# Modulation jobs moved out of the first and last attention head, beside values and Fourier inputs

## What is computed

```python
def adaln(cond, w_mod, b_mod):
    m = jax.nn.silu(cond) @ w_mod + b_mod
    return jnp.split(m, 3, axis=-1)
...
def attn_fourier_layer(...):
    shift, scale, gate = adaln(c, w_mod, b_mod)
    h = rmsnorm(x, norm_g) * (1.0 + scale[:, None]) + shift[:, None]
    q, k, v, f, z = jnp.split(h @ w_in, SPLIT0, axis=-1)
    q = apply_rope(q.reshape(B, S, N_Q_HEADS, HEAD_DIM), cos, sin)
    ...
    y = jnp.concatenate([windowed_attention(q, k, v, kc, vc, sink), fourier_mix(f, w_f)], axis=-1)
    x = x + gate[:, None] * ((y * jax.nn.silu(z)) @ w_out)
...
def pool_layer(...):
    shift, scale, gate = adaln(c, w_mod, b_mod)
    h = rmsnorm(x, norm_g) * (1.0 + scale[:, None]) + shift[:, None]
    x = x + gate[:, None] * pool_branch(h, w_in, w_grp, layer_scale, w_out)
```

## Time and profile before

| | us |
|---|---|
| median of 3 executions | 1515.44 (1514.88 to 1517.31) |
| the profiled execution | 1516.59 |
| its span, first to last instruction | 1514.9 |
| PE busy | 1440.4 (95%) |
| DVE busy | 888.8 (59%) |
| ACT busy | 499.5 (33%) |
| mean granted clock of PE | 0.986 |

### The profile page before, as it was taken

The page is one execution under the profiler, slowest core; times in us unless marked ns, Lnnn a source line. Parts: engine busy times, 40 slices in busy tenths (PEclk is TensorE's granted clock), DMA queues, the critical chain, the costliest instruction groups (busy, mean ns, idle before and its releaser), DMA issues.

```text
span 1514.9 us, 18270 instructions
## 1 busy us (share of the span) xinstructions
PE 1440.4 (95%) x6822; PEld 1166.2 (77%) x6822; DVE 888.8 (59%) x1389; ACT 499.5 (33%) x732; POOL 85.4 (6%) x159
## 2 busy tenths in 40 slices
PE   4799999999998999998999999999999999999995
PEld 0366888888877788877788888888888888888884
DVE  3643444436666868686755577655554666674433
ACT  3332332325544534344322244111252222332221
POOL 1000000000000000000010000000000000010001
PEclk9899999999999999999999999999999999999997
DMA  9777346545642333333475666533333322365322
GB/s 389 294 278 282 124 127 195 182 140 184 194 133 72 123 98 126 94 127 111 166 237 185 193 193 193 167 98 98 97 98 97 98 87 94 98 190 198 101 70 111
DMA packets 63684, 232.57 MB, mean 154 GB/s; under 512 B 7104, under 2 KB 8000, under 8 KB 62336
## 3 DMA queue, kind: packets, MB, share of 16 engines
q1 hardware_dynamic: 40896, 145.77, 29.3%
q0 software_dynamic: 21040, 80.42, 16.3%
q10 hardware_dynamic: 1680, 5.43, 1.0%
HBM read 227.40 MB, written 4.19 MB: 153 GB/s over the span
## 4 chain that ended last, share of the span: by engine, by line
PE 84%; DVE 9%; DMA 2%; issue 1%; ACT 1%; POOL 0%; DVEq 0%; SPq 0%; ACTq 0%; POOLq 0%
PE ps L1235 83%; DMA raw<-in_mod 2%; DVE w_lo L746 2%; PE ps L1447 1%; DVE stat L998 1%; DVE pt_lo L1019 1%; DVE tmp L846 1%; DVE modchunk L753 1%; DVE main L791 1%; DVE h_lo L798 1%; DVE h_lo L800 1%; DVE kvmem L874 0%; DVE kvmem L1025 0%; ACT scratch L507 0%; DVE main L849 0%
## 5 line engine op out<-in xcount | busy, mean ns | idle before, releaser
L1235 PE MATMUL ps<-h_hi,w_hi 128*128 128x512 f32 x1600 | 635.0, 397 | 6.5 <-DVE h_lo L800 5.9
L1235 PE MATMUL ps<-h_hi,w_lo 128*128 128x512 f32 x1600 | 625.8, 391 | 0.0
L1235 PE MATMUL ps<-h_lo,w_hi 128*128 128x512 f32 x1600 | 625.5, 391 | 0.0
L746 DVE TENSOR_TENSOR w_lo<-raw,w_hi 128x1024 fp32r<-128x1024 f32 x208 | 254.6, 1224 | 404.4 <-ACT w_hi L410 403.9
L410 ACT CAST w_hi<-raw 128x1024 fp32r<-128x1024 f32 x208 | 218.1, 1049 | 651.8 <-PE ps L1235 651.7
L1235 PEld LDWEIGHTS ps<-h_hi,w_hi 128*128 128x128 f32 x1600 | 302.6, 189 | 81.4 <-issue 22.3
L1235 PEld LDWEIGHTS ps<-h_hi,w_lo 128*128 128x128 f32 x1600 | 301.9, 189 | 64.2
L1235 PEld LDWEIGHTS ps<-h_lo,w_hi 128*128 128x128 f32 x1600 | 302.4, 189 | 60.1 <-issue 0.2
L753 DVE CUSTOM_DVE_ANT_0 modchunk<-modchunk,cond_row 128x1024 f32<-128x1024 f32 x128 | 155.3, 1219 | 2.5 <-DMA modchunk<-in_modb 2.5
L357 POOL DMA_DIRECT2D modchunk<-in_modb x128 | 67.6, 528 | 1171.8 <-DVE modacc L753 1138.7
L611 ACT CAST pt_hi<-ps 128x512 fp32r<-128x512 f32 (+1 forms) x48 | 30.7, 640 | 129.9 <-PE ps L1447 129.8
(11 more groups left out here) (199 smaller groups left out, 1378.1 us busy)
## 6 DMA issues: line engine op xcount, KB each, us to landing
raw<-in_weights SPq DMA_DIRECT2D x208, 512.0 KB, 3.5
modchunk<-in_modb POOLq DMA_DIRECT2D x128, 512.0 KB, 4.3
raw<-in_mod SPq DMA_DIRECT2D x44, 512.0 KB, 5.4
modchunk<-in_mod SPq DMA_DIRECT2D x20, 512.0 KB, 4.9
main<-in_xT POOLq DMA_DIRECT2D x4, 1024.0 KB, 13.3
kvmem<-in_weights POOLq DMA_DIRECT2D x8, 512.0 KB, 5.4
main<-in_xT ACTq DMA_DIRECT2D x4, 1024.0 KB, 4.8
out<-main SPq DMA_DIRECT2D x12, 256.0 KB, 3.1
```

Source lines behind the costliest of these rows:

```text
L746: nc.vector.tensor_tensor(w_lo[:, j % 2], src, w_hi[:, j % 2].bitcast(F32), ALU.subtract).then_inc(lo_ready, 1)
L1235: return nc.tensor.matmul(out, lhsT, rhs, start=start, stop=stop, skip_group_check=True)
```

## The change

On DVE the sets beside values and Fourier inputs become two each, so two jobs stand in each unit, one after the other, and the first and the last head have none. The sets keep their order. In the first head the third part of a rotation stands with the second, one slot earlier. In the last head the splits move, on ACT and on DVE, from behind the slot's cast to its end. The number of instructions of each kind stays as it was.

```diff
--- before.py
+++ after.py
@@ -64,7 +64,7 @@
 BANKS = ([LOWER, (6, 7, 4, 5), (2, 3, 0, 1), UPPER, LOWER, UPPER] + [LOWER] * 4 + [UPPER, LOWER] * 8)
 POOL_BANKS = (UPPER, LOWER, UPPER, LOWER)
 
-M_V, M_F, M_Q, M_Z, M_O, M_U, M_O1, M_END = starts(1, 1, 3, 4, 4, 1, 2)
+M_V, M_F, M_Q, M_Z, M_O, M_U, M_O1, M_END = starts(2, 2, 3, 2, 4, 1, 2)
 
 H_X, H_MIX0, H_L1, H_MIX1 = starts(2 * KT, KT, KT)
 
@@ -598,9 +598,6 @@
                     if k in UNIT_SLOTS:
                         s = UNIT_SLOTS.index(k)
                         hi(i + G_Z, s + 2)
-                        if last and 2 * s < EARLY:
-                            split(H_MIX0 + 2 * s, main[:, 2 * s], h_hi[:, 2 * s])
-                            split(H_MIX0 + 2 * s + 1, main[:, 2 * s + 1], h_hi[:, 2 * s + 1])
                     if k in QUERY_SLOTS:
                         n = QUERY_SLOTS.index(k) + 1
                         if n >= 2:
@@ -618,6 +615,9 @@
                     if first and k % 3 == 1 and k < 3 * GROUP:
                         m = k // 3
                         swap(3 * GROUP + m, main[:, 3 * GROUP + m], scratch, 3 * GROUP + m)
+                    if last and k in UNIT_SLOTS and UNIT_SLOTS.index(k) < EARLY // 2:
+                        for t in (2 * UNIT_SLOTS.index(k), 2 * UNIT_SLOTS.index(k) + 1):
+                            split(H_MIX0 + t, main[:, t], h_hi[:, t])
                     if last and k in (7, 10, 13):
                         reload_x((7, 10, 13).index(k))
                     if k == STEPS and not last:
@@ -762,17 +762,23 @@
                 nc.vector.tensor_tensor(modv_flat[:, bass.ds(cg * GROUP, GROUP)], modsum[:],
                                         vec[:, bass.ds(cg * GROUP + V_BMB, GROUP)], ALU.add).then_inc(modv_ready, 1)
 
-            def group(n, cg=None, finish=None, side=None, last=False):
+            def jobs(cg, sets, s):
+
+                for f in range(sets * s, sets * (s + 1)):
+                    job(cg + f // HALVES, f % HALVES)
+                    if f % HALVES == HALVES - 1:
+                        reduced(cg + f // HALVES)
+
+            def group(n, cg=None, finish=None, side=None, last=False, sets=1):
 
                 for s in range(HALVES - 1 if not last else HALVES - 2):
                     lo(n, s + 2)
                     if cg is not None:
-                        job(cg, s)
+                        jobs(cg, sets, s)
                     if side:
                         side(s)
                 if cg is not None:
-                    job(cg, HALVES - 1)
-                    reduced(cg)
+                    jobs(cg, sets, HALVES - 1)
                 if finish:
                     finish()
                 if not last:
@@ -956,8 +962,8 @@
             lo(G_K, HALVES + 1)
             dve.wait_ge(rope_landed, 32)
             dve.wait_ge(cond_row_ready, 2)
-            group(G_V, M_V, finish_values, side=rotate_beside(0, lambda m: keys[:, m]))
-            group(G_F, M_F)
+            group(G_V, M_V, finish_values, side=rotate_beside(0, lambda m: keys[:, m]), sets=2)
+            group(G_F, M_F, sets=2)
             nc.vector.memset(folded[:, :, 1, 0:1], 0.0)
             fold(0)
             fold(1)
@@ -1005,9 +1011,6 @@
                     if k in UNIT_SLOTS:
                         s = UNIT_SLOTS.index(k)
                         lo(i + G_Z, s + 2)
-                        if last and 2 * s < EARLY:
-                            split(H_MIX0 + 2 * s, main[:, 2 * s], h_hi[:, 2 * s], h_lo[:, 2 * s])
-                            split(H_MIX0 + 2 * s + 1, main[:, 2 * s + 1], h_hi[:, 2 * s + 1], h_lo[:, 2 * s + 1])
                     if k in QUERY_SLOTS:
                         n = QUERY_SLOTS.index(k) + 1
                         piece(i * PIECES + (5 + n), q_lo[:, n % 2],
@@ -1024,14 +1027,19 @@
                         p = probs[par][:, 0:width - 1]
                         nc.vector.tensor_scalar(p, p, stat[:, 3, par:par + 1], None,
                                                 ALU.mult).then_inc(probs_ready, 1)
-                    if k in JOB_SLOTS:
-                        job(i + M_Z, JOB_SLOTS.index(k))
+                    if k in JOB_SLOTS and not (first or last):
+                        job(i + (M_Z - 1), JOB_SLOTS.index(k))
+                    if last and k in UNIT_SLOTS and UNIT_SLOTS.index(k) < EARLY // 2:
+                        for t in (2 * UNIT_SLOTS.index(k), 2 * UNIT_SLOTS.index(k) + 1):
+                            split(H_MIX0 + t, main[:, t], h_hi[:, t], h_lo[:, t])
                     if first and 2 <= k:
                         m, part = divmod(k - 2, 3)
-                        rotate_part(3 * GROUP + m, main[:, 3 * GROUP + m], scratch[:], part)
+                        for turn in ((0,), (1, 2), ())[part]:
+                            rotate_part(3 * GROUP + m, main[:, 3 * GROUP + m], scratch[:], turn)
                     if k == STEPS and not last:
                         keys_and_first_queries(i + 1)
-                reduced(i + M_Z)
+                if not (first or last):
+                    reduced(i + (M_Z - 1))
                 dve.wait_ge(y_done, i * BLOCKS + BLOCKS)
                 if last:
                     lo(i + G_Z, HALVES + 1)
```

## The result

The changed kernel takes 1505.9 us (median of 4, 1504.6 to 1507.2) against 1515.9 us: the ratio is 0.9935, with a 95% interval from 0.9923 to 0.9947. The forecast was 1506.8 us. Its profiled execution took 1507.1 us, with a span of 1505.5. The gain is small, 0.65%, but clear of the noise.

The account below looks back on a forecast made before the run. TensorE (PE) was taken as the bound, busy nearly throughout. Heads -19.7 us and added work beside values and Fourier inputs +11.1 us give -8.6 us: median 1515.4 to 1506.8 us, range 1499.5 to 1514.5.

Parts of the forecast that it names:

- Swaps in the first head: First head: ACT's last three swaps no longer wait for DVE's add, so PE stalls shrink by 1.5, 2.65 and 2.0 us.
- The low part at slot 7 and the head's end: First head: PE's 0.58 us stall for the probabilities' low part and 1.33 us before the second head end: 0.6, 1.3 us.
- Splits in the last head: Last head: with splits behind the scaling, PE's waits for it fall from 5.0 to 1.25 us; a 0.8 us wait goes.
- Jobs behind the scaling worth nothing: Last head: the eight jobs leaving it stand ahead of maxima that PE does not wait for, so they gain nothing.
- The clock: First and last head: with large stalls gone, all 7.1 us lost at clock 0.96 are regained; the other end is zero.
- The values stage: Near 236 us: another job pair delays the first context-values copy, and PE waits for its bank, +1.9 us.
- The Fourier stage: Near 286 us: job pairs outlast units, lateness piles up, and PE waits for the second query unit's low part, +6.65 us.
- the cycle of a pair: Fourier stage: job start to issue 2.0 us plus landing 4.5 us, so 6.5 us against a unit of 5.44 us.
- The queues' share: Fourier stage: DMA queue use rises from 0.58 to 0.73, not full, which spoke against lengthening landings.
- Slow clock behind it: After the values and Fourier stalls: slow-clock stretches cost 0.8 and 1.75 us, together +2.55 us.
- D: Rival, chance 0.13: Fourier-stage landings lengthen under their own traffic; gain gone at 5.7 us, 1519.4 us at 6.3.
- B: Rival, chance 0.15: loads keep up, landing in 3.8 us, a pair in 5.8 us; added cost 4.45 us, time 1500.2 us.

## Why the prediction was right, step by step

- **Swaps in the first head**: -1.5, -2.65, -2.0 us forecast; the three stalls became 0, 0.43 and 0. Shown by the rotation part alone.
- **The low part at slot 7 and the head's end**: -0.6 and -1.3; both stalls are gone. The first went with the jobs alone and with the rotation part alone, so that either was enough; the forecast gave it to the job. Of the second, the rotation part alone left 1.18 of 1.33 us and the jobs alone left none, so there it was the job, not the add, that mattered.
- **Splits in the last head**: 5.0 to 1.25 us forecast, 0.9 measured. The quarter of a microsecond that I put on a wait coming back did not come. Shown by the splits alone.
- **Jobs behind the scaling worth nothing**: PE's wait for the scaling fell from 5.0 to 4.2 us with the jobs alone. In slots 2 and 8 of the kernel before the maximum starts right behind a job, and with the jobs alone DVE is idle for 0.6 us before it; the waits of 0.63 and 1.06 us behind these two became 0.20 and 0.65. The splits' move removes these waits by itself (0.9 us with the jobs still there), so the zero did no harm to the sum.
- **The clock**: 7.1 us forecast. Both heads had a clock of 1.00 in the first profile; in the second the first head had 0.98, one low stretch that cost 1.6 us. The sum holds within that; the reasoning "a stall of this size, so a slow stretch" is too simple. With jobs or rotation moved alone the last head kept stalls of 1.78 and 1.54 us at a clock of 1.00, and 1.79 us at the start of the first head brought a slow stretch in some kernels and none in others. What decides it stays open.
- **The values stage**: +1.9 forecast, 1.0 and 1.2 measured in two profiles of the changed kernel, 1.5 to 1.7 in others with two sets there.
- **The Fourier stage**: +6.65 forecast, 4.2 and 5.4 measured. The place, the waiting instruction and the cause were as said; the mis-sized term is the cycle of a pair, 6.2 us in the first profile and 6.4 in the second instead of 6.5. Over seven cycles 0.3 us are 2.1 of the 2.4 us by which the forecast was above the first profile. The cycle was issue and landing and nothing else: 1.9 us to the issue, where I took 2.0, and in the first profile a landing of 4.2 us on average, where I took 4.5. The median of all landings of the stage, 3.8, is lower than that, because the loads of the other half, which did not set the pace, were shorter on average. The queues' share, 0.73 forecast, was 0.73 and 0.70.
- **Slow clock behind it**: +2.55 forecast; a clock of 0.59 over 7 us is work lost for 2.9 us, and the stretch of the ledger less its two stalls gives 8.67 - 1.01 - 4.23 = 3.4 us, and 8.74 - 1.23 - 5.40 = 2.1 us in the second pair. The longer stall had the shorter slow stretch, so the whole row repeated to 0.1 us; no run shows why.
- **The rivals**: the balance of D needed landings of 5.7 us; the mean was 4.2 where it mattered. B needed a pair in 5.8 us; the median landing was as short as B had it, but those of the half that set the pace were not, so the stall stayed. The warning of the Trainium skill (SBUF — State Buffer, "SBUF: two separate sides") about descriptors held up by a DVE instruction that holds the shared port did not show; whether a job holds that port is in no row. POOL's issues took 0.53 us, and the landings behind them had a median of 3.8 us. The Trainium skill's formula for a load (DMA: Bandwidth & Descriptors, section "Anatomy of one DMA — SWDGE (gpsimd) path"), by which I estimated 3.2 us for 512 KB, lies below the 3.6 us of the shortest landing in that stage.

What the forecast did not ask was which part of the change earns the gain, though its own terms answer it: it charged 11.1 us to the moved jobs and gave them 1.9 us of stalls in the heads. The job moves, which the change is named for, cost 2.7 us by themselves (1518.3 against 1515.6) and 6.9 us on top of the two reorderings.

## What to carry to other kernels

On an engine that works in order, look at what stands ahead of the instruction that another engine's queue waits for: standing a 0.7 us add one slot earlier, for each of four tiles, gave 10 us. A swap that waited for the add had held up the instructions behind it that PE needed; the stalls that went sum to 7 us, and the rest is the clock. Work that waits for a load is not free on an idle engine: with two buffers the cycle is job to issue and landing, and the queue of the engine where one forms, and if that is longer than a unit, the lateness comes out at the end of the stage. When a change bundles moves, price each one alone; here the best version, 1495.0 us, keeps the small reorderings, leaves the bulk of the work where it was, and moves a single job.

## What the hardware showed that I had not expected

- Landings of 512 KB on POOL's queue became shorter under more traffic: median 3.8 us at a queue share of 0.73, against 4.3 us at 0.58 with one load per unit. The weight loads beside them went the other way, from a median of 3.5 to one of 4.2 us. The first two pairs, issued 1.1 and 1.2 us apart, took 3.8 to 4.6 us; later ones, issued 2.2 to 3.6 us apart, mostly 3.6 to 4.0 us. But single loads, issued 5.4 us apart, had taken 4.0 to 4.3 us, so distance alone does not explain it, and the cause stays open.
- Stalls of 1.5 to 1.8 us were followed by the lower clock in some kernels and not in others, in the same place with the same stall to 0.1 us. Two profiles of the kernel before agreed in all four places of the heads; of the changed kernel, the second had a low stretch at the start of the first head and the first had none.
- The opening, the same code in all kernels, ended between 158.5 and 160.7 us.
